# Counting the four narrowest tiles of a threshold search on GpSimd, and splitting the other ten anew

## The chip, the cores and the metric

The kernel runs on one core of a Trainium2 chip. The metric is the device time of one execution in microseconds: the median of three runs is 4006.64 us (4005.96 to 4007.17).

## The reference, cut to what matters

One inference step of a decoder layer. Part of it is a sparse attention: for every one of the prompt's 2048 queries a score is computed for each earlier key, and only the 256 keys with the highest scores are attended.

```python
score = jnp.einsum('bth,bths->bts', wi, jax.nn.relu(dots)).astype(jnp.float32)
causal = jnp.arange(L)[None, :] <= q_pos[:, None]
score = jnp.where(causal[None], score, -jnp.inf)
vals, sel = lax.top_k(score, topk)          # topk = 256
valid = vals > -jnp.inf
```

A second group of queries (8 sequences of 8 queries, the samples) attends 256 of 8192 cached positions; its keys and values are gathered from a paged cache. The layer also has a gated linear recurrence, projections and an MLP, which this change leaves alone.

## The kernel before

**How the search works.** The prompt's queries lie in 16 tiles of 128, one query per partition. The scores of tile i are a row of (i+1) x 128 columns in `score` (float32, in SBUF). The first two tiles need no selection. For the other 14 (widths 384 to 2048) the kernel looks, for each query, for the largest float whose bits, set one by one from the top, still leave at least 256 scores at or above it. That takes 32 rounds (`ROUNDS`). In each round every tile is compared with its candidate and the hits are counted; then the bit is kept or dropped, and the next candidate is formed.

Two engines count. VectorE does it in one `tensor_scalar` (`is_ge`, with the sum as `accum_out`, L2865). ACT does it in one `activation` with `Sign` and the sum (L2788). `split_search` divides the tiles by a cost table: VectorE has the widths 2048, 1792, 1536, 1280, 896, 640, 512 (8704 columns), ACT 1920, 1408, 1024, 384, 1664, 1152, 768 (8320 columns). The tiles lie in two halves, `GROUPS`. When a half is counted, VectorE's `update(r, g)` waits for both engines' counts, keeps or drops the bit (L2848, L2849), writes the candidates of the next round (L2851) and raises `cand_rdy[g]`. So one half is counted while the other is updated.

**What it is interleaved with.** The 32 rounds run inside `attend_sample_and_search_prompt`, which attends the samples. It goes over four pairs of sequences in five phases. Each phase has 16 steps (`NCK`). In a step TensorE turns key rows (L2681), multiplies queries by them (L2689), adds a mask (L2696), turns the probabilities of the pair before (L2718) and multiplies them by the values (L2732). Phase 0 has no probabilities yet and phase 4 has no keys any more. ACT copies every turned block out of PSUM (L2802) and takes the exponentials (L2809); VectorE moves the logits out with their maximum (L2907).

Each engine has its own program in order. The search is a generator in each of them. The list `STEPS` (10.0 for the start, then 5.4, 6.6 and 4.9 per step) says how much of the 32 rounds stands in each step: `step_of(position)` gives the step of a position counted in rounds, and `search_until(step)` issues all counts that are due up to that step. Counted so, phase 0 holds 5.62 rounds, phases 1 to 3 hold 6.87 each, and phase 4 holds 5.10.

**GpSimd's queue.** GpSimd has only the gathers of key and value rows (L2646), 64 in all, into four key buffers and four value buffers. A key gather waits until TensorE has turned the rows that lay in its buffer (`t_done`), and a value gather until TensorE has multiplied by its own (`t_used`, which `logits` and `times_v` raise, and `times_new` doesn't).

The stage behind, `mark_prompt_and_recur_sample`, uses the same split of tiles. There VectorE first counts ACT's tiles again, against the next float above (L1757), before ACT marks the chosen keys.

## Time and profile before

| | |
|---|---|
| median of three runs | 4006.64 us |
| the profiled execution | 4005.41 us |
| its span | 4003.6 us |
| TensorE, VectorE, ACT, GpSimd busy | 3559.9, 2780.9, 2215.1, 1054.2 us |
| stage of the search, first to last count | 1349 to 1818 us |
| L2865, VectorE's counts, over the span | 328.5 us |
| L2788, ACT's counts, over the span | 286.4 us |

The span is the time from the first to the last instruction of the profiled execution; the execution itself took 1.8 us more. Busy times of different engines overlap. A line such as L2865 is a line of the kernel before. A releaser ("<-ACT turned L2802") is what ended an engine's idle time. GpSimd is called POOL in the rows, and VectorE DVE.

### The profile page before, as it was taken

How to read it: one execution, taken by the hardware profiler on the slowest of the kernel's cores; microseconds unless marked ns; L12 is line 12 of the kernel's file. 1: busy time of each engine (PE TensorE's matmuls, PEld its weight loads, DVE VectorE, ACT ScalarE, POOL GpSimd, SP SyncE). 2: the span in 40 equal slices, each digit the busy share in tenths (PEclk: the TensorE clock that was granted, in tenths of full speed). 3: DMA queues.
4: the chain of work that ended last, by engine and by line, in shares of the span. 5: the costliest groups of instructions: out<-in, count | busy, mean ns of one | idle time of the engine just before them, and what ended most of it. 6: DMA issues, size and time to landing. Idle time of an engine off the chain costs nothing. (4 is left out here: it accounts for less than half of the span.)

```text
span 4003.6 us, 53467 instructions
## 1 busy us (share of the span) xinstructions
PE 3559.9 (89%) x18410; PEld 2847.4 (71%) x18411; DVE 2780.9 (69%) x4729; ACT 2215.1 (55%) x3701; POOL 1054.2 (26%) x1140
## 2 busy tenths in 40 slices
PE   8999999879777489874699999979999998999998
PEld 7778787778555245453588887868888887888886
DVE  6675756878888789798678885665565554555565
ACT  4343424766678599897577774345455443433232
POOL 0000001755210011110256730216555551000011
PEclk9999999999878699995799999989999999999999
DMA  6555454555100244423456633576677666554464
GB/s 169 180 149 163 144 162 128 156 152 145 44 22 16 93 153 164 159 97 117 126 196 226 233 133 130 201 238 198 200 229 225 187 192 189 184 179 152 137 218 137
DMA packets 394575, 633.11 MB, mean 158 GB/s; under 512 B 98073, under 2 KB 220793, under 8 KB 386009
## 3 DMA queue, kind: packets, MB, share of 16 engines
q1 hardware_dynamic: 314712, 314.14, 26.3%
q0 software_dynamic: 79200, 315.79, 23.7%
q8 instruction: 138, 2.26, 0.2%
q14 instruction: 109, 0.89, 0.1%
q10 hardware_dynamic: 416, 0.02, 0.0%
HBM read 448.87 MB, written 180.96 MB: 157 GB/s over the span
## 5 line engine op out<-in xcount | busy, mean ns | idle before, releaser
L3890 PE MATMUL up_acc<-x_parts_first,w_up_parts 128*128 128x512 f32 x1536 | 358.7, 393 | 15.1 <-DVE w_up_parts L3638 15.1
L775 PE MATMUL accumulated<-hT,w_in_parts 128*128 128x512 f32 x1536 | 360.4, 394 | 3.2 <-DVE w_in_parts L509 3.2
L3890 PEld LDWEIGHTS up_acc<-x_parts_first,w_up_parts 128*128 128x128 f32 x1536 | 291.4, 190 | 77.0 <-DVE w_up_parts L3638 16.0
L775 PEld LDWEIGHTS accumulated<-hT,w_in_parts 128*128 128x128 f32 x1536 | 289.9, 190 | 66.2 <-DVE w_in_parts L509 4.9
L2865 DVE TENSOR_SCALAR_CACHE_REDUCE junk_dve<-score,candidate 128x2048 bf16<-128x2048 f32 (+6 forms) x224 | 328.5, 1505 | 8.8 <-DVE candidate L2851 8.3
L3983 PE MATMUL down_acc<-w_down_parts_even,hidden_parts 128*128 128x512 f32 x1344 | 316.6, 393 | 13.2 <-DVE hidden_parts L3674 10.8
L3983 PE MATMUL down_acc<-w_down_parts_odd,hidden_parts 128*128 128x512 f32 x1344 | 312.7, 390 | 0.0
L3983 PEld LDWEIGHTS down_acc<-w_down_parts_even,hidden_parts 128*128 128x128 f32 x1344 | 254.6, 190 | 67.8 <-issue 14.8
L2788 ACT ACTIVATE junk_act<-score,candidate 128x1920 bf16<-128x1920 f32 (+6 forms) x224 | 286.4, 1294 | 21.2 <-DVEq L2852 17.4
L3436 ACT ACTIVATE hidden_parts<-hidden_raw 128x1024 fp32r<-128x1024 f32 x112 | 118.6, 1059 | 311.7 <-PE down_acc L3983 289.5
L3983 PEld LDWEIGHTS down_acc<-w_down_parts_odd,hidden_parts 128*128 128x128 f32 x1344 | 251.9, 188 | 53.1 <-issue 1.0
L357 ACT ACTIVATE w_in_parts<-w_in_raw 128x1024 fp32r<-128x1024 f32 (+1 forms) x112 | 113.6, 1014 | 290.7 <-PE accumulated L771 120.9
L509 DVE TENSOR_TENSOR w_in_parts<-w_in_raw,w_in_parts 128x1024 fp32r<-128x1024 f32 (+1 forms) x112 | 130.8, 1169 | 198.1 <-ACT w_in_parts L357 197.1
L3638 DVE TENSOR_TENSOR w_up_parts<-up_raw,w_up_parts 128x512 fp32r<-128x512 f32 x224 | 176.0, 786 | 113.8 <-ACT w_up_parts L3414 112.3
L771 PE MATMUL accumulated<-w_in_parts,hT 128*128 128x512 f32 (+1 forms) x1152 | 239.4, 366 | 1.7 <-DVE hT L530 1.7
L2173 DVE TENSOR_TENSOR probs_T<-p_T,probs_T 128x512 fp32r<-128x512 f32 x272 | 183.9, 688 | 72.6 <-ACT probs_T L2097 71.3
L771 PEld LDWEIGHTS accumulated<-w_in_parts,hT 128*128 128x128 f32 x1152 | 200.2, 188 | 32.2 <-issue 3.2
L3674 DVE TENSOR_TENSOR hidden_parts<-hidden_raw,hidden_parts 128x1024 fp32r<-128x1024 f32 x112 | 138.1, 1233 | 112.3 <-ACT hidden_parts L3436 112.0
L2097 ACT ACTIVATE probs_T<-p_T 128x512 fp32r<-128x512 f32 x272 | 157.0, 594 | 94.0 <-PE p_T L2033 93.0
L1449 PE MATMUL dots<-ki_high,qi_parts 128*128 128x512 f32 (+3 forms) x304 | 146.5, 483 | 70.0 <-ACT relu L1471 68.2
L3333 POOL DMA_DIRECT2D hidden_raw<-scratch_hs x112 | 59.8, 534 | 538.1 <-DVE hidden_parts L3674 538.1
L1518 DVE SCALAR_TENSOR_TENSOR score<-relu,wi,score 128x1024 f32<-128x1024 f32 (+7 forms) x154 | 180.5, 1172 | 24.7 <-ACT relu L1471 7.6
(556 smaller groups left out, 8655.7 us busy)
## 6 DMA issues: line engine op xcount, KB each, us to landing
hidden_raw<-scratch_hs POOLq DMA_DIRECT2D x112, 512.0 KB, 4.5
w_in_raw<-in_w_in SPq DMA_DIRECT2D x80, 512.0 KB, 4.1
up_raw<-scratch_ws SPq DMA_DIRECT2D x128, 256.0 KB, 3.0
scratch_hs<-hidden_even POOLq DMA_DIRECT2D x112, 256.0 KB, 4.9
scratch_hs<-hidden_odd POOLq DMA_DIRECT2D x112, 256.0 KB, 4.8
up_raw<-in_w_up SPq DMA_DIRECT2D x96, 256.0 KB, 5.7
weight_sums<-in_w_down POOLq DMA_DIRECT2D x16, 1024.0 KB, 5.3
scratch_wt<-weight_sums POOLq DMA_DIRECT2D x16, 1024.0 KB, 5.8
```

The costliest lines, as they stand in the source:

```text
L771: mm = pe.matmul(z, h[:, a, k, n * P:(n + 1) * P], w2[:, g % 2, b, k2 * w:(k2 + 1) * w], start=(first and j == 0), stop=(last and j == 2))
L775: mm = pe.matmul(z, w2[:, g % 2, b, k2 * ST + n * P:k2 * ST + (n + 1) * P], h[:, a, k, :], start=(first and j == 0), stop=(last and j == 2))
L1449: pe.matmul(dots[:, u % DB, c:c + w], qs[:, b, h, :], kh[:, k], start=True, stop=False)
L1518: dve.scalar_tensor_tensor(s, r, wi[:, i, h:h + 1], s, ALU.mult, ALU.add).then_inc(acc_done, 1)
L2097: act.activation(ET[:, s % 3, 0, :], pT[:, turn_at[s] % 3, :], ACT.Copy).then_inc(th_rdy, 1)
L2173: dve.tensor_tensor(ET[:, s % 3, 1, :], pT[:, turn_at[s] % 3, :], ET[:, s % 3, 0, :].bitcast(F32), ALU.subtract).then_inc(tl_rdy, 1)
L2788: act.activation(ja[:, n % 2, 0:WIDTH[i]], score[:, SOFF[i]:SOFF[i + 1]], ACT.Sign, bias=cf[:, c:c + 1], accum_out=cnt[:, c:c + 1]).then_i ...
L2865: dve.tensor_scalar(jd[:, n % 2, 0:WIDTH[i]], score[:, SOFF[i]:SOFF[i + 1]], cf[:, c:c + 1], None, ALU.is_ge, ALU.add, accum_out=cnt[:, c: ...
L3638: dve.tensor_tensor(out, raw[:, g % RAW, :], high.bitcast(F32), ALU.subtract).then_inc(lo_rdy, 1)
L3674: dve.tensor_tensor(ap[:, s % A_PARTS, 1, :], araw[:, s % A_RAW, :], ap[:, s % A_PARTS, 0, :].bitcast(F32), ALU.subtract).then_inc(a_lo, 1)
L3890: mm = pe.matmul(up_bank(n), wp[:, n % SLOTS, b, q * P:(q + 1) * P], X(i)[:, a, q, :], start=(q == 0 and (a, b) == (0, 0)), stop=(q == QUA ...
L3983: mm = pe.matmul(down_bank(s), ap[:, s % A_PARTS, a, j * P:(j + 1) * P], B(ph)[:, j, b, :], start=(j == 0 and (a, b) == (0, 0)), stop=(j = ...
```

## The change

The four narrowest tiles (768, 384, 640 and 512 columns, in this order) go to GpSimd. [...] It writes the comparison's zeros and ones as bf16 (`reaches_pool`), adds the right half of the row to the left half, halves what is left again, and writes the last sum, 64 to 96 columns wide, to `counts_pool`. VectorE's `update` reduces these to a count with a new `tensor_reduce`, in both halves. The other ten tiles are split by a new cost rule: ACT gets 2048, 1792, 1920 and 1664 (7424 columns), VectorE 1536, 1408, 1280, 1152, 1024 and 896 (7296 columns). In GpSimd's program the counts that are due up to a step stand ahead of the key gather that waits for that step.

```diff
+POOL_TILES = 4
 def split_search():
-    cost, mine = {"dve": 4400.0, "act": 5500.0}, {"dve": [], "act": []}
-    for i in sorted(SEARCHED, key=lambda i: -WIDTH[i]):
-        t = {"dve": 1.12 * WIDTH[i] + 110, "act": 0.97 * WIDTH[i] + 190}
-        who = min(t, key=lambda e: cost[e] + t[e])
-        cost[who] += t[who]
-        mine[who].append(i)
-    return mine["dve"], mine["act"][0::2] + mine["act"][1::2]
+    narrow = sorted(SEARCHED, key=lambda i: WIDTH[i])[:POOL_TILES]
+    pool = narrow[-1:] + narrow[:1] + narrow[1:-1][::-1]
+    wide = sorted((i for i in SEARCHED if i not in pool), key=lambda i: -WIDTH[i])
+
+    def share(n):
+        return max(3850 + sum(0.833 * WIDTH[i] + 308 for i in wide[:n]),
+                   2800 + sum(1.042 * WIDTH[i] + 209 for i in wide[n:]))
+
+    n = min(range(2, len(wide) - 1), key=share)
+    return wide[n:], wide[:n][0::2] + wide[:n][1::2], pool
...
+        ADDED = (slice(0, half_pt), slice(NSRCH - half_pt, NSRCH))
+        ENDS = {i: WIDTH[i] >> (3 if WIDTH[i] >= 512 else 2) for i in PT}
+        reaches = sb("reaches_pool", [P, max(WIDTH[i] for i in PT)], BF16)
+        part = sb("counts_pool", [P, len(PT), max(ENDS.values())], BF16)
...
+                link_p = Chain(pool, chain_p)
+
+                def counts():
+                    link_p(pool.memset(part[:, :, :], 0.0))
+                    for r in range(ROUNDS):
+                        for m, i in enumerate(PT):
+                            yield step_of(r + m / len(PT))
+                            c, w = col[i], WIDTH[i]
+                            if m % half_pt == 0:
+                                pool.wait_ge(cand_rdy[m // half_pt], r + 1)
+                            pool.wait_ge(p_cnt, len(PT) * r + m)
+                            link_p(pool.tensor_scalar(reaches[:, 0:w], score[:, SOFF[i]:SOFF[i + 1]], cf[:, c:c + 1], None, ALU.is_ge))
+                            while w > 2 * ENDS[i]:
+                                w //= 2
+                                link_p(pool.tensor_tensor(reaches[:, 0:w], reaches[:, 0:w], reaches[:, w:2 * w], ALU.add))
+                            w //= 2
+                            pool.tensor_tensor(part[:, m, 0:w], reaches[:, 0:w], reaches[:, w:2 * w], ALU.add).then_inc(p_cnt, 1)
...
                 for n in range(4 * NS + 2 * LASTP):
+                    if n >= KB:
+                        pair, c, s = place(n - KB)
+                        search_until(NCK * pair + 4 * c + 3)
                     if n < 4 * NS:
                         if n >= KB:
-                            pair, c, s = place(n - KB)
                             pool.wait_ge(t_done, ev_k(pair, 4 * c + 3, s) + 1)
...
+                search_until(len(STEPS) - 1)
...
                     dve.wait_ge(a_cnt, na * r + (n1, na)[g])
+                    dve.wait_ge(p_cnt, len(PT) * r + half_pt * (g + 1))
+                    link_c(dve.tensor_reduce(cnt[:, ADDED[g]], part[:, half_pt * g:half_pt * (g + 1), :], AX.X, ALU.add))
```

`Chain` raises a semaphore with each instruction and waits for it, so each of GpSimd's instructions waits for the one before. In the rows below, GpSimd's lines are L2646 for a gather before, and after the change L2657 for a gather, L2670 for the compare, L2673 for a halving and L2675 for the last addition of a tile.

GpSimd at the end of the stage, before: the last gathers follow each other with nothing between them.

```order
L2646 DMA k_rows<-in_cache_k,gather_kv 128x2048
L2646 DMA v_rowsS<-in_cache_v,gather_kv 128x2048
L2646 DMA k_rows<-in_cache_k,gather_kv 128x2048
L2646 DMA v_rowsS<-in_cache_v,gather_kv 128x2048
```

And after the change, the last two gathers (of value rows) with the end of the counts in front of them and the beginning of those behind them.

```order
L2673 TENSOR_TENSOR reaches_pool<-reaches_pool 128x192
L2675 TENSOR_TENSOR counts_pool<-reaches_pool 128x96
L2670 TENSOR_SCALAR reaches_pool<-score,candidate 128x384
L2673 TENSOR_TENSOR reaches_pool<-reaches_pool 128x192
L2675 TENSOR_TENSOR counts_pool<-reaches_pool 128x96
L2657 DMA v_rowsS<-in_cache_v,gather_kv 128x2048 x2
L2670 TENSOR_SCALAR reaches_pool<-score,candidate 128x640
L2673 TENSOR_TENSOR reaches_pool<-reaches_pool 128x320
L2673 TENSOR_TENSOR reaches_pool<-reaches_pool 128x160
L2675 TENSOR_TENSOR counts_pool<-reaches_pool 128x80
L2670 TENSOR_SCALAR reaches_pool<-score,candidate 128x512
```

The gathers now stand between counts. Of the last three pairs of value gathers, the first has 5 tiles' counts behind it up to the second, the second 5 up to the third, and the third 10 up to the end: 20 tiles, which are 5 rounds. A pair of key and value gathers in the phases before has 6 or 7 tiles' counts up to the next group of four gathers.

VectorE over one round in phase 0, before, between two of the maxima of L2907.

```order
L2907 TENSOR_SCALAR logitsS,z_max<-zL 128x512
L2865 TENSOR_SCALAR junk_dve,count<-score,candidate 128x1280
L2848 TENSOR_TENSOR kept<-count,least_count 128x7
L2849 COPY_PREDICATED F<-kept,candidate 128x7
L2851 TENSOR_TENSOR candidate<-F,bits_p 128x7
L2865 TENSOR_SCALAR junk_dve,count<-score,candidate 128x896
L2907 TENSOR_SCALAR logitsS,z_max<-zL 128x512
```

And the same place after the change, where L2948 is the maximum, L2906 a count and L2881 the new reduction.

```order
L2948 TENSOR_SCALAR logitsS,z_max<-zL 128x512
L2881 TENSOR_REDUCE count<-counts_pool 128x2
L2889 TENSOR_TENSOR kept<-count,least_count 128x6
L2890 COPY_PREDICATED F<-kept,candidate 128x6
L2892 TENSOR_TENSOR candidate<-F,bits_p 128x6
L2906 TENSOR_SCALAR junk_dve,count<-score,candidate 128x1152
L2906 TENSOR_SCALAR junk_dve,count<-score,candidate 128x1024
L2948 TENSOR_SCALAR logitsS,z_max<-zL 128x512
```

The update begins with the reduction of GpSimd's partial sums, so VectorE's queue now also waits for GpSimd there; the maxima stand behind it.

## Rows read from the trace of the kernel before

**Rows 1.** The page's chain that ended last, by line.

```profile
PE down_acc L3983 15%; PE up_acc L3890 14%; PE out_acc L3956 4%; PE sample_acc L3915 1%; PE mix_turned L3859 0%; PE sample_acc L3931 0%; PE sample_turned L3931 0%; DVE x_parts_first L3638 0%; PE rows_turned L3868 0%; DMA down_raw<-scratch_wt 0%; DMA hidden_raw<-scratch_hs 0%; DVE x_parts_last L3638 0%; DMA up_raw<-scratch_ws 0%; PE sample_turned L3902 0%; DMA scratch_xc<-normed_T 0%
```

**Rows 2.** Busy time by stretch: the five phases (start:end, length, engines).

```profile
1363.00:1443.60 80.60, 62.89 (x225) 24.61 (x225) 68.81 (x144) 62.01 (x103) 11.24 (x12) 0.85 0.43 156
1443.60:1541.90 98.30, 88.90 (x546) 51.10 (x546) 88.18 (x178) 93.14 (x153) 14.72 (x16) 0.97 0.41 150
1541.90:1642.50 100.60, 90.71 (x563) 52.44 (x560) 89.27 (x183) 92.88 (x153) 12.44 (x14) 0.97 0.44 165
1642.50:1754.30 111.80, 92.55 (x547) 51.83 (x545) 88.77 (x180) 93.42 (x151) 12.18 (x13) 0.94 0.34 123
1754.30:1818.70 64.40, 44.57 (x329) 35.95 (x329) 60.21 (x118) 61.23 (x98) 5.62 (x6) 0.84 0.27 99
```

**Rows 3.** Timeline of TensorE, value products of two successive steps (start, us).

```profile
1522.76 1.58 PE L2732 MATMUL zO<-v_rowsS,turned 128*64 128x128 f32 x16
...
1528.21 1.58 PE L2732 MATMUL zO<-v_rowsS,turned 128*64 128x128 f32 x16
```

**Rows 4.** Timeline of TensorE at a phase's end (in brackets: idle before).

```profile
1541.63 0.43 PE L2745 MATMUL zO<-v_new,turned 8*64 8x128 f32 x4 [3.15 <-ACT turned L2802]
```

**Rows 5.** Waits in the stage: us in total, times, longest.

```profile
PE zL L2689 <- ACT turned L2802: 36.8, 28, 4.0
```

**Rows 6.** Groups by form in the stage, counts (busy us, mean ns).

```profile
L2865 DVE TENSOR_SCALAR_CACHE_REDUCE junk_dve<-score,candidate 128x2048 bf16<-128x2048 f32 x32 | 74.9, 2342 | 0.3 <-DVE candidate L2856 0.3
...
L2865 DVE TENSOR_SCALAR_CACHE_REDUCE junk_dve<-score,candidate 128x512 bf16<-128x512 f32 x32 | 23.7, 742 | 0.0
...
L2788 ACT ACTIVATE junk_act<-score,candidate 128x1920 bf16<-128x1920 f32 x32 | 60.9, 1905 | 18.2 <-DVEq L2852 14.5 <-DVEq L2858 3.7
...
L2788 ACT ACTIVATE junk_act<-score,candidate 128x384 bf16<-128x384 f32 x32 | 20.0, 626 | 0.0
```

**Rows 7.** The same view, VectorE's reduction of 128 elements.

```profile
L2925 DVE TENSOR_REDUCE z_max<-logitsS 128x1 f32<-128x128 f32 x4 | 1.1, 286 | 0.1
```

**Rows 8.** Timeline of VectorE: first instruction of an update, and the count behind it.

```profile
1523.79 0.17 DVE L2848 TENSOR_TENSOR kept<-count,least_count 128x7 int32<-128x7 f32 x1
...
1524.53 1.15 DVE L2865 TENSOR_SCALAR_CACHE_REDUCE junk_dve<-score,candidate 128x896 bf16<-128x896 f32 x1 [0.17 <-DVE candidate L2851]
```

**Rows 9.** GpSimd's instructions elsewhere (min/median/max ns; memsets: busy us, ns).

```profile
L1424 POOL CAST qi_parts<-qi_rows x12: 1040/1142/1728, 1024.5 to 1247.1; 128x1024 fp32r<-128x1024 f32 x12
...
L1948 POOL TENSOR_TENSOR weight_sums<-weight_sums x16: 1272/1282/1294, 1979.2 to 2168.7; 128x512 f32<-128x512 f32 x16
...
L1426 POOL TENSOR_TENSOR qi_parts<-qi_rows,qi_parts x12: 2363/2572/3096, 1025.7 to 1248.6; 64x1024 fp32r<-64x1024 f32 x12
...
L989 POOL TENSOR_TENSOR less_ref<-r_b,b_less_log_k x96: 620/836/1280, 684.5 to 862.9; 128x256 f32<-128x256 f32 x96
...
L1620 POOL MEMSET minus_twos<- 128x2048 bf16 x1 | 1.8, 1795 | 0.0
...
L994 POOL MEMSET qi_blocks<- 128x1024 f32 x1 | 0.9, 945 | 0.0
...
L995 POOL MEMSET ki_new<- 128x64 f32 x1 | 0.1, 145 | 0.0
```

**Rows 10.** Timeline of GpSimd: two additions of which the second waits for the first.

```profile
1981.72 1.28 POOL L1961 TENSOR_TENSOR weight_sums<-weight_sums 128x512 f32<-128x512 f32 x1
1983.08 1.29 POOL L1963 TENSOR_TENSOR weight_sums<-weight_sums 128x512 f32<-128x512 f32 x1
```

**Rows 11.** Timeline of GpSimd: gathers of value rows in the last phase.

```profile
1764.40 0.94 POOL L2646 DMA_INDIRECT v_rowsS<-in_cache_v,gather_kv  x1 [27.86 <-PE zO L2732]
1765.64 0.94 POOL L2646 DMA_INDIRECT v_rowsS<-in_cache_v,gather_kv  x1 [0.30 <-issue]
...
1799.33 0.94 POOL L2646 DMA_INDIRECT v_rowsS<-in_cache_v,gather_kv  x1 [13.74 <-PE zO L2732]
```

**Rows 12.** Timeline of ACT in the stage behind: its first mark.

```profile
1841.01 0.72 ACT L1673 ACTIVATE sides<-score,minus_last 128x512 bf16<-128x512 f32 x1
```

More of the change, by code:

```diff
@@ L1267, with search_columns @@
 SOFF = [o - OFF[FIRST] for o in OFF]
+POOL_TILES = 4
 def split_search():
-    cost, mine = {"dve": 4400.0, "act": 5500.0}, {"dve": [], "act": []}
-    for i in sorted(SEARCHED, key=lambda i: -WIDTH[i]):
-        t = {"dve": 1.12 * WIDTH[i] + 110, "act": 0.97 * WIDTH[i] + 190}
-        who = min(t, key=lambda e: cost[e] + t[e])
-        cost[who] += t[who]
-        mine[who].append(i)
-    return mine["dve"], mine["act"][0::2] + mine["act"][1::2]
-def search_columns(dt, at):
-    nd0 = (len(dt) - 1) // 2
-    return nd0, dt[:nd0] + at + dt[nd0:]
+    narrow = sorted(SEARCHED, key=lambda i: WIDTH[i])[:POOL_TILES]
[6 more added lines that the diff above has]
+    return wide[n:], wide[:n][0::2] + wide[:n][1::2], pool
+def search_columns(dt, at, pool):
+    nd0, half = (len(dt) - 1) // 2, len(pool) // 2
+    return nd0, half + nd0, pool[:half] + dt[:nd0] + at + dt[nd0:] + pool[half:]
 PROBS_SKIP = 136000
@@ L1537, in mark_prompt_and_recur_sample @@
     LV = 3
-    DT, AT_ = split_search()
-    nd, columns = search_columns(DT, AT_)
+    DT, AT_, PT = split_search()
+    _, nd, columns = search_columns(DT, AT_, PT)
     ACTS = slice(nd, nd + len(AT_))
@@ L2564, in attend_sample_and_search_prompt @@
         o_done, o_rdy, out, chain = sem("z_o"), sem("z_or"), sem("z_out"), sem("z_chain")
-        DT, AT_ = split_search()
-        nd, na = len(DT), len(AT_)
+        DT, AT_, PT = split_search()
+        nd, na, half_pt = len(DT), len(AT_), len(PT) // 2
         n1 = -(-na // 2)
-        nd0, columns = search_columns(DT, AT_)
+        nd0, a0, columns = search_columns(DT, AT_, PT)
         col = {i: n for n, i in enumerate(columns)}
-        GROUPS = (slice(0, nd0 + n1), slice(nd0 + n1, NSRCH))
-        SIGNED = (slice(nd0, nd0 + n1), slice(nd0 + n1, nd0 + na))
+        GROUPS = (slice(0, a0 + n1), slice(a0 + n1, NSRCH))
+        SIGNED = (slice(a0, a0 + n1), slice(a0 + n1, a0 + na))
+        ADDED = (slice(0, half_pt), slice(NSRCH - half_pt, NSRCH))
+        ENDS = {i: WIDTH[i] >> (3 if WIDTH[i] >= 512 else 2) for i in PT}
+        reaches = sb("reaches_pool", [P, max(WIDTH[i] for i in PT)], BF16)
+        part = sb("counts_pool", [P, len(PT), max(ENDS.values())], BF16)
+        p_cnt, chain_p = sem("z_p_cnt"), sem("z_chain_p")
         F, flip = keep["F"], keep["flip"]
@@ L2647, in gather, with search_until @@
                                             bass.IndirectOffsetOnAxis(ap=gkv[:, 2 * pair + s, c:c + 1], axis=0)).then_inc(done[g % nb], 16)
+                link_p = Chain(pool, chain_p)
[14 more added lines that the diff above has]
+                            pool.tensor_tensor(part[:, m, 0:w], reaches[:, 0:w], reaches[:, w:2 * w], ALU.add).then_inc(p_cnt, 1)
+                search = counts()
+                due = [next(search)]
+                def search_until(step):
+                    while due[0] <= step:
+                        due[0] = next(search, len(STEPS))
                 for n in range(4 * NS + 2 * LASTP):
+                    if n >= KB:
+                        pair, c, s = place(n - KB)
+                        search_until(NCK * pair + 4 * c + 3)
                     if n < 4 * NS:
                         if n >= KB:
-                            pair, c, s = place(n - KB)
                             pool.wait_ge(t_done, ev_k(pair, 4 * c + 3, s) + 1)
@@ L2872, in rounds @@
                     update(ROUNDS - 1, 1)
-                    link_c(dve.tensor_tensor(F[:, nd0:nd0 + na], F[:, nd0:nd0 + na], bitn[:, 31:32].to_broadcast([P, na]), ALU.bitwise_xor))
+                    link_c(dve.tensor_tensor(F[:, a0:a0 + na], F[:, a0:a0 + na], bitn[:, 31:32].to_broadcast([P, na]), ALU.bitwise_xor))
                 search = rounds()
@@ L4021, in constants @@
     second = np.stack([np.tile(a, (1, RH)) for a in halves], 1).astype(np.int32)
-    dt_, at_ = split_search()
-    least = [2 * TOPK - 1 - WIDTH[i] if i in at_ else TOPK for i in search_columns(dt_, at_)[1]]
+    dt_, at_, pt_ = split_search()
+    least = [2 * TOPK - 1 - WIDTH[i] if i in at_ else TOPK for i in search_columns(dt_, at_, pt_)[2]]
     bits = np.array([1 << b for b in range(30, -1, -1)] + [0], np.uint32)
```

## The prediction

> **What bounds the kernel now.** I read the chain of waits first: its two longest items are lines of the MLP at the kernel's end, far from this change [rows 1]. Nothing there alters, so the change is worth what the stage that holds the search, `attend_sample_and_search_prompt`, becomes shorter or longer, and everything behind it shifts. Then I cut that stage into five stretches at the ends of its pair phases [rows 2]. By the table STEPS they hold 5.62, 6.87, 6.87, 6.87 and 5.10 search rounds (0.65 lies before, hidden by the loads of the queries). The reader is to see that no engine has room: in the three middle stretches VectorE is busy for 88 to 89 us, ACT for 93 and TensorE for 89 to 93, of 98.3, 100.6 and 111.8.
>
> The timeline of TensorE gives its floor: one middle step, from one block of 16 value products to the next, takes 5.45 us with no gap [rows 3]. Sixteen steps are 87.2 us; the idle gaps at a phase's end (3.15 us before its last product [rows 4], about as long again for the first exponential) lift that to about 94.5. So TensorE alone forbids a middle stretch under 94.5, and the most the change could save there is 4 + 6 + 17 = 27 us. The last two stretches are long because TensorE waits for ACT's copies: 36.8 us in the stage before L2689 alone [rows 5].
>
> The table by form gives the counts [rows 6]. VectorE: 2342 ns at 2048 columns and 742 at 512, so 1.042 ns a column and 209 ns; the next starts 0.075 us early, at the accumulator read. ACT: 1905 at 1920 and 626 at 384, so 0.833 ns a column and 306 ns.
>
> **The change part by part.** VectorE counts 7296 columns in 6 instructions instead of 8704 in 7: 10.5 - 0.5 = 10.0 us a round become 8.86 - 0.45 = 8.4. Each of the two updates a round gains one reduction of 2 x 96 elements. One over 128 elements took 286 ns [rows 7]; at 1.04 ns an element this is 0.36 us, 0.40 with the gap, 0.8 a round. The update itself takes 0.74 us, from 1523.79 to 1524.53 [rows 8], as before. VectorE's round goes from 11.5 to 10.7. ACT counts 7424 columns in 4 instructions instead of 8320 in 7: 9.0 us become 7.4.
>
> In the second stretch VectorE's busy 88.2 us lose 6.87 x 0.8 = 5.5 and become 83, and ACT's 93.1 lose 6.87 x 1.65 = 11 and become 82 [rows 2]. Both fall well under TensorE's 94.5.
>
> GpSimd gets 15 instructions a round, none of a kind seen in this trace. Compares: 4 over 2304 columns with one input. The nearest rows are the cast, 1040 ns at least over 1024, and the memsets, 145 ns over 64 and 945 over 1024 [rows 9]: 0.833 ns a column and 0.19 us each, 2.7 us. Adds: 11 over 1968 columns with two inputs. A row of 512 columns takes 1282 ns; at 2.50 ns a column and nothing fixed they are 4.9 us. Through it and 2363 ns (1024 columns of half the partitions) the line is 2.11 a column and 0.2 us, 6.35 in all. I take 5.8, since something fixed is in every row. Each instruction waits for the one before; such a pair stood 0.08 us apart, from 1983.00 to 1983.08 [rows 10]: 1.2 us. A round is 9.7 us. From both sides: adds at the one-input rate give 3.7 and a round of 7.6; compares at the two-input rate give 5.7 and a round of 13.2. I take 9.7 because the cast is the nearest row to a compare.
>
> The Trainium skill (GPSIMD Engine Reference, Performance pitfalls for Q7 kernels) says that a body that produces a truth value costs 2.03 cycles an element if it isn't unrolled and 1.03 if it is. The trace has only the cast's rate. At its 1.2 GHz that would be, as an estimate, 1.7 ns a column, and a round of 11.7 us.
>
> GpSimd also issues the gathers, 1.24 us each from start to start [rows 11]. Four middle steps hold 1.72 rounds and 4 gathers: 1.72 x 9.7 + 5.0 = 21.7 us against 24 of a quarter stretch. It fits, with 2 us to spare. But the queue is in order, and that is the new wait. Before a key gather stand all counts up to that step; behind it a value gather waits until TensorE has used its buffer, and behind that wait stand the counts of the next four steps. VectorE's update waits for them, and behind it in its queue stand the maxima that TensorE's logits need, and the candidates that ACT waits for. In the second stretch the value gather is free about 2 us after VectorE enters the last step that GpSimd has counted for, so nothing is lost. `times_new` doesn't raise `t_used`, so each later phase's gathers are released one event later: in the third and fourth stretches by logits of the following step. There GpSimd starts its counts about 3 us late; its quarter stays at 24 to 25 us.
>
> Sum by stretch. First: VectorE's 5.62 rounds lose 0.8 each, and GpSimd's 5.62 x 9.7 + 12 x 1.24 = 69.4 us fit into 76; 80.6 becomes 76, -4.5. Second: TensorE's floor and 1.5 us, -2.3. Third: 97.5, -3. Fourth: ACT's share of a step falls by 0.43 x 1.65 = 0.7 us, 16 of them 11 us, of which the late counts take 1: -10.
>
> Last stretch: here the queue costs. By the rows the gathers left at 10.1 us into it (1764.40) and at 45.0 us (1799.33), in step with TensorE [rows 11], and VectorE searched on meanwhile. Now the first of them has exactly 5 rounds of counts behind it (order shown with the change: 5 tiles, 5 tiles, 10 tiles). From 10.1 us on GpSimd needs 5 x 9.7 = 48.5 us, 6 gathers of 1.24, 7.4 us, and sits out two waits in which ACT alone goes on for up to 0.64 rounds. In the first ACT has two tiles to count once the second half's candidates are there, then a copy and the product: 3.4 us after GpSimd is done. In the second ACT needs one tile more, 5.0 us. With the final update 0.8: 75.2 us against 64.4, +10.8.
>
> Total: -4.5 - 2.3 - 3 - 10 + 10.8 = -9. The stage behind counts ACT's tiles again, 4 instead of 7; ACT started its marks there at 1841.01 with no idle time before it [rows 12], behind its own activations and not behind these counts, so I take 0. `memset` of the partial sums ahead of the first gather, some 0.4 us by the memsets' line, hides behind the load of the queries. The profiled execution took 4005.4 us (span 4003.6); the median is 4006.6, 1.2 above. So 3996.4 + 1.2: 3997 us.
>
> **Rivals.** (a) GpSimd is cheap, 8 us a round, since bf16 adds may be nearer to the one-input rate. The stretches save 5, 3.3, 5 and 13 us and the last loses only 10.8 - 5.3 x 1.7 = 1.8: 3982. For it: the output and inputs of the adds are half as wide as in any row. Against: the bf16 memset ran at the f32 memset's rate.
> (b) Slower: GpSimd becomes the bound. The place is its quarter of a middle stretch; it decides from (24 - 5) / 1.72 = 11 us a round. At 12 us a quarter is 25.6 and a middle stretch 102.4 + 3 for the phase's end: +7, +5 and -6; the first +3, the last 10.8 + 5.3 x 2.3 = +23. Total +32: 4039. For it: compares have no row, and all 15 instructions wait on each other. Against: it needs compares at nearly twice the cast's rate.
> (c) GpSimd and VectorE hold each other up. L989 took 620 ns at least, 836 as median and up to 1280 [rows 9], so other work can stretch it by a third. All of GpSimd's work a third longer is 8.5 x 1.35 + 1.2 = 12.7 us a round, +50: 4057. Against: VectorE's counts read one tensor at one column per 1.04 ns, and L1948 stayed at 1272 to 1294 ns for all 16. The Trainium skill (GPSIMD Engine Reference, Key points) puts contention on VectorE instructions in a two-port mode or with two SBUF inputs; by that rule only the small ones of the updates would meet it.
> (d) Gains and the loss at the end cancel within the measurement: 4006.
>
> **How the numbers follow.** What a measurement tells from no change is 0.2%, 8 us. The forecast, 0.45, has 3984 to 4012 as its own range, since the four savings rest on waits that could each be off by 2 to 3 us: 0.28 of it faster, 0.12 same, 0.05 slower. (a) 0.17, faster. (b) 0.26, slower. (c) 0.07, slower. (d) 0.05, same. Together faster 0.45, same 0.17, slower 0.38. The range goes from 3972, a little under (a), to 4045, a little over (b); the bound of 13.2 us a round, some +65 us, stays outside with most of (c).
>
> **What would show it.** GpSimd's instructions from one 768-column compare to the next, without gathers: 9.7 us, compares 0.83 and adds about 2.3 ns a column. VectorE 8.4 and ACT 7.4 us of counts a round. Three middle stretches of 96 to 102 us with TensorE's gaps before L2689 in the stage under 25 us. A last stretch of about 75 us, ended by GpSimd's counts, with VectorE idle before the new reductions. If that stretch is no longer than 65 us, the step on the queue is wrong; if a round of GpSimd is over 11 us, the price is.

## The result and the profile after

The changed kernel took 4086.58 us (median of 4 runs, 4083.68 to 4096.2) against 4006.89 of the kernel before on the same chip (4005.96 to 4007.17): 1.0202 times as long (95% interval 1.0189 to 1.0216). Forecast were 3997 us in a range of 3972 to 4045. The change makes the kernel slower by 80 us, more than the 50 of the dearest rival, and the time lies outside the range. A GpSimd round over 11 us was named as the sign that the price is wrong; it is 14.05 us, as shown below. The profiled execution took 4083.68 us, 78.3 more than the one before, with a span of 4081.9 and a mean granted clock of 0.93 (0.937 before).

The five stretches of the stage in the changed kernel, cut as in [rows 2] (start:end, length, then busy us of PE, PEld, DVE, ACT and POOL, the granted clock, DMA share and GB/s):

```profile
1363.00:1447.30 84.30, 60.68 (x225) 23.68 (x223) 67.20 (x144) 55.11 (x73) 72.45 (x87) 0.86 0.28 105
1447.30:1563.10 115.80, 95.45 (x554) 53.66 (x554) 86.40 (x179) 82.65 (x111) 102.39 (x119) 0.88 0.38 146
1563.10:1679.70 116.60, 94.36 (x554) 52.49 (x554) 86.88 (x182) 83.43 (x112) 102.86 (x121) 0.91 0.38 145
1679.70:1794.10 114.40, 90.59 (x549) 51.09 (x547) 87.98 (x183) 83.16 (x111) 101.11 (x120) 0.97 0.34 130
1794.10:1893.60 99.50, 48.07 (x325) 39.14 (x325) 59.99 (x116) 53.97 (x65) 71.97 (x85) 0.71 0.18 64
```

The stage starts at the same 1363.00, and its five stretches are 3.7, 17.5, 16.0, 2.6 and 35.1 us longer: 74.9 of the 78.3. ACT lost the 10 us a stretch that it was meant to lose (93.1 to 82.7 in the second), and is no bound. The engine that has filled up is GpSimd: 102 busy us of 116, where it had 12 to 15; most of the rest are the gaps of about 0.09 us between instructions that wait for each other. The granted clock of the second stretch fell from 0.97 to 0.88 and that of the last from 0.84 to 0.71, while TensorE waited more; the second stretch holds nearly the same matmuls (554 and 546 records), and their busy time rose from 88.90 to 95.45 us. The fourth stretch is nearly as long (114.4 us) with the clock at 0.97 and 90.59 busy us, so the clock isn't what makes these stretches long.

One round of GpSimd without a gather, from one compare of 768 columns to the next (start, us):

```profile
1350.22 2.21 POOL L2670 TENSOR_SCALAR reaches_pool<-score,candidate 128x768 bf16<-128x768 f32 x1 [0.16 <-issue]
1352.52 1.53 POOL L2673 TENSOR_TENSOR reaches_pool<-reaches_pool 128x384 bf16<-128x384 bf16 x2
...
1364.27 2.20 POOL L2670 TENSOR_SCALAR reaches_pool<-score,candidate 128x768 bf16<-128x768 f32 x1 [0.17 <-POOL counts_pool L2675]
```

It takes 14.05 us, not 9.7. The groups by form say which part of it is dearer (busy us, mean ns | idle before):

```profile
L2670 POOL TENSOR_SCALAR reaches_pool<-score,candidate 128x768 bf16<-128x768 f32 x32 | 70.5, 2203 | 4.9 <-POOL counts_pool L2675 4.6 <-issue 0.2
...
L2670 POOL TENSOR_SCALAR reaches_pool<-score,candidate 128x384 bf16<-128x384 f32 x32 | 39.8, 1244 | 2.8
...
L2673 POOL TENSOR_TENSOR reaches_pool<-reaches_pool 128x384 bf16<-128x384 bf16 x32 | 29.2, 912 | 2.7
```

The additions are as forecast: 5.7 us a round, where I took 5.8. Through the two compares the line is (2203 - 1244) / 384 = 2.50 ns a column and 0.28 us fixed; all of them are 220.6 us x128, so 6.9 us a round. Forecast were 2.7, from a line through the cast's 1040 ns with the memsets' slope of 0.833 ns a column [rows 9]. That alone is 4.2 of the 4.35 us that a round is longer.

The waits of the stage (us in total, times, longest) name what follows from it:

```profile
ACT junk_act L2827 <- DVEq L2893: 117.3, 48, 9.5
...
DVE count L2881 <- POOL counts_pool L2675: 114.9, 39, 9.9
...
PE zL L2728 <- ACT turned L2841: 68.0, 31, 7.4
```

VectorE waits 115 us for the partial sums, ACT 117 for the new candidates that VectorE gives out only then, and TensorE's wait for ACT's copies went from 36.8 [rows 5] to 68.0. The last shows under ACT's name. But in ACT's program the copies stand behind its counts, and the counts waited for candidates: whoever reads only the last releaser would blame the engine that was relieved.

### The profile page after: what moved, and what is told of

The parts are those of the page before. It is cut to its first block and busy times, and to the rows that moved or that the text cites. A ratio compares the mean times of both kernels' runs of the same rounds, so it can differ in the third digit from the quotient of the medians.

```text
span 4081.9 us, 53818 instructions
## 1 busy us (share of the span) xinstructions
PE 3565.5 (87%) x18411; PEld 2846.9 (70%) x18411; DVE 2772.5 (68%) x4723; ACT 2168.7 (53%) x3509; POOL 1462.6 (36%) x1621
## 3 DMA queue, kind: packets, MB, share of 16 engines
q0 software_dynamic: 79200, 315.79, 23.1%
## 5 line engine op out<-in xcount | busy, mean ns | idle before, releaser
L2827 ACT ACTIVATE junk_act<-score,candidate 128x2048 bf16<-128x2048 f32 (+3 forms) x128 | 235.1, 1838 | 121.1 <-DVEq L2893 117.3
L2906 DVE TENSOR_SCALAR_CACHE_REDUCE junk_dve<-score,candidate 128x1536 bf16<-128x1536 f32 (+2 forms) x192 | 276.9, 1476 | 7.0 <-DVE candidate L2892 6.5
L2670 POOL TENSOR_SCALAR reaches_pool<-score,candidate 128x768 bf16<-128x768 f32 (+3 forms) x128 | 220.6, 1723 | 18.2 <-POOL counts_pool L2675 8.9
L2728 PE MATMUL zL<-turned,q_blocks 128*64 128x512 f32 x256 | 151.3, 692 | 73.5 <-ACT turned L2841 68.0
```

Of the source, the lines that this page charges most:

```text
L2670: link_p(pool.tensor_scalar(reaches[:, 0:w], score[:, SOFF[i]:SOFF[i + 1]], cf[:, c:c + 1], None, ALU.is_ge))
L2728: pe.matmul(lp[half(s), n % 2, :], qb[:, 2 * pair + s, :], turned[:, e % TB, :], start=True, stop=False, skip_group_check=True).then_inc(t ...
L2827: act.activation(ja[:, n % 2, 0:WIDTH[i]], score[:, SOFF[i]:SOFF[i + 1]], ACT.Sign, bias=cf[:, c:c + 1], accum_out=cnt[:, c:c + 1]).then_i ...
L2906: dve.tensor_scalar(jd[:, n % 2, 0:WIDTH[i]], score[:, SOFF[i]:SOFF[i + 1]], cf[:, c:c + 1], None, ALU.is_ge, ALU.add, accum_out=cnt[:, c: ...
```

## The experiments

Two theories stood at first. **A**: a compare is slow by itself on GpSimd. **B** (rival): it is slow because VectorE reads the same scores beside it, as in rival (c). And a second question: would the forecast hold if the compare had the price that I gave it?

**e1_alone: the forms of instruction with VectorE standing still.** Ahead of the counts GpSimd runs nine forms at 768 and at 384 columns, and VectorE starts its search only behind them. Added; nothing is left out, and the total says nothing:

```
+ for w in (768, 384):
+     row = score[:, 0:w]
+     link_p(pool.tensor_scalar(reaches[:, 0:w], row, thr[:, 0:1], None, ALU.is_ge))
+     ... # against a constant, subtract, f32 output, bf16 input, add and multiply,
+     ... # a copy, bf16 addition, f32 addition
+ pool.sem_inc(alone, 1)
  ...
+ dve.wait_ge(alone, 1)
```

> The changed kernel with 18 extra GpSimd instructions ahead of the first gather, while VectorE, ACT and TensorE wait: nine forms at 768 and at 384 columns, each behind the one before. Theory: GpSimd's compare costs 2.5 ns a column by itself, 2.20 us at 768 and 1.24 us at 384 as in the changed kernel, and a plain copy about 0.83 to 1.0 ns a column; then the price that failed is the comparison's (or that of any one-input arithmetic: subtract at 2.5 as well would say that). Rival, contention with VectorE: alone the compare takes 1.5 us or less at 768. The total time of this run says nothing but for its extra 15 to 30 us.

Timeline of GpSimd: compare, subtract, add and multiply by constants, copy; then the compare of 384:

```profile
1353.05 2.21 POOL L2668 TENSOR_SCALAR reaches_pool<-score,least_count 128x768 bf16<-128x768 f32 x1
...
1357.58 2.21 POOL L2670 TENSOR_SCALAR reaches_pool<-score,least_count 128x768 bf16<-128x768 f32 x1
...
1364.47 0.83 POOL L2673 TENSOR_SCALAR reaches_pool<-score 128x768 bf16<-128x768 f32 x1
1365.37 0.82 POOL L2674 CAST reaches_pool<-score 128x768 bf16<-128x768 f32 x1
...
1369.89 1.25 POOL L2668 TENSOR_SCALAR reaches_pool<-score,least_count 128x384 bf16<-128x384 f32 x1
```

2.21 us alone (VectorE is idle from 1348.88 to 1379.85 us) against 2.203 in the kernel, 1.25 against 1.244: the price is the instruction's own, and contention on GpSimd's side is out. Theory A held. It isn't a matter of types either (bf16 input 2.20, f32 output 2.21), nor of the truth value, since a subtraction costs the same; against a constant it is 2.13.

**e7_forms: is it the column of scalars, or the number of operations?** e1 left open why one form of the same instruction ran at 0.83. The same place, with nine other forms:

```
+ tensor_scalar(..., row, thr[:, 0:1], 1.0, ALU.is_ge, ALU.mult)
+ tensor_scalar(..., row, thr[:, 0:1], 2.0, ALU.subtract, ALU.mult)
+ tensor_scalar(..., row, 2.0, thr[:, 0:1], ALU.mult, ALU.add)
+ tensor_scalar(..., row, 0.5, thr[:, 0:1], ALU.add, ALU.mult)
+ tensor_scalar(..., row, 2.0, None, ALU.mult)
+ ... # four more
```

> As e1_alone, with other forms of GpSimd's tensor_scalar at 768 and 384 columns: two operations in one instruction (compare and multiply, subtract and multiply, multiply and add, subtract and compare) and one multiplication. In e1_alone one operation cost 2.5 ns a column whatever it was, but add and multiply with two constants 0.85. Theory A: it is the number of operations, and compare with a multiplication by 1 is fast too, about 0.83 us at 768. Theory B: only multiply with add has a fast path, and every form with a compare stays at 2.2 us at 768.

Timeline of GpSimd, the five forms above in their order:

```profile
1350.56 2.86 POOL L2668 TENSOR_SCALAR reaches_pool<-score,least_count 128x768 bf16<-128x768 f32 x1
...
1356.39 2.86 POOL L2670 TENSOR_SCALAR reaches_pool<-score,least_count 128x768 bf16<-128x768 f32 x1
1359.35 0.91 POOL L2671 TENSOR_SCALAR reaches_pool<-score,least_count 128x768 bf16<-128x768 f32 x1
...
1363.31 0.90 POOL L2673 TENSOR_SCALAR reaches_pool<-score,least_count 128x768 bf16<-128x768 f32 x1
...
1367.25 2.15 POOL L2675 TENSOR_SCALAR reaches_pool<-score 128x768 bf16<-128x768 f32 x1
```

Neither. A multiplication and an addition together, in either order, run at the cast's rate, even with a column of scalars. Every other form that was tried is slow, a single multiplication too (2.15), and a compare or a subtraction with a second operation takes 2.86. A single addition was not tried. A compare has no form among those tried that runs at the rate I assumed.

**e2_short_compare: the round at the price that I had forecast.** Each compare reads only `ENDS` of its tile's columns (64 to 96, the width at which the additions end), so that the round is near 9.7 us with every instruction, wait and addition in place. Left out: the rest of the four narrowest tiles' columns; their thresholds come from an eighth to a quarter of them, and the number of hits asked for is scaled to that. The last addition of a tile takes the short compare's output as one input. The core of the edit:

```
- link_p(pool.tensor_scalar(reaches[:, 0:w], score[:, SOFF[i]:SOFF[i + 1]], ..., ALU.is_ge))
+ e = ENDS[i]
+ link_p(pool.tensor_scalar(some[:, 0:e], score[:, SOFF[i]:SOFF[i] + e], ..., ALU.is_ge))
```

> The changed kernel with GpSimd's compares cut to the last sum's width (64 to 96 columns instead of 384 to 768), all additions left in and the least counts scaled to it; so the four narrowest tiles get thresholds from a part of their columns. GpSimd's round falls from 14.0 to about 9.1 us, near the 9.7 of the prediction. Theory (only the price of the compare was wrong): the stretches come out as the prediction's sum, the middle ones 96 to 102 us, the last about 73, and the total 3990 to 4003. Rival (the queue with the gathers, or the new wait of the update, costs by itself): middle stretches stay over 104 us, and the total over 4012.

Busy time by stretch, second to last:

```profile
1440.70:1536.80 96.10, 89.85 (x554) 51.82 (x554) 82.74 (x178) 82.47 (x111) 67.72 (x118) 0.96 0.46 173
1536.80:1632.60 95.80, 89.85 (x552) 51.78 (x553) 84.32 (x183) 83.35 (x111) 68.83 (x121) 0.96 0.47 176
1632.60:1738.80 106.20, 91.43 (x550) 51.35 (x548) 85.95 (x183) 82.89 (x111) 64.94 (x115) 0.95 0.38 140
1738.80:1821.90 83.10, 44.44 (x325) 36.15 (x325) 59.28 (x116) 53.90 (x65) 44.69 (x81) 0.79 0.21 77
```

Its round is 9.1 us, 0.6 under the 9.7 of the forecast. 4010.30 us, ratio 1.0011 (1.0001 to 1.0020). So the price of the compare is worth about 76 us of the 80 lost. But the kernel doesn't get to 3997 either, nor into the 3990 to 4003 expected of this run: neither theory came out whole. The second and third stretches are as forecast (96.1 and 95.8 for 96 and 97.5) with TensorE's clock back at 0.96; the fourth is 4 us over (106.2 for 102), and the last, forecast at 75.2 with a longer round, is 83.1.

**e3_two_tiles: half of it moved.** `POOL_TILES = 4` becomes 2: GpSimd counts only the tiles of 512 and 384 columns, ACT five and VectorE seven. Nothing is left out.

> The changed kernel with two tiles (512 and 384 columns) on GpSimd instead of four; ACT then has five tiles with 8960 columns, VectorE seven with 7168. GpSimd's round is about 5.9 us by the measured instructions (3.3 + 2.5), a quarter of a middle stretch 15 us of 24, so it is no bound. Theory: VectorE's round is 8.4 + 1.5 + 0.6 = 10.5 us instead of 11.5, ACT's stays at 8.9; the time comes back to 3990 to 4012, with a last stretch lengthened by the gathers' waits by some 3 us. Rival (any count behind the gathers costs): over 4020.

The last two stretches:

```profile
1633.20:1745.40 112.20, 94.84 (x554) 53.53 (x554) 81.79 (x193) 92.16 (x124) 46.48 (x59) 0.92 0.36 132
1745.40:1818.60 73.20, 44.90 (x329) 36.03 (x329) 56.39 (x131) 62.53 (x78) 31.61 (x41) 0.86 0.24 87
```

4003.61 us, ratio 0.9994 (0.9982 to 1.0005): the loss is gone, a gain isn't there. That is inside the expected 3990 to 4012. The last stretch is 8.8 us longer than before, where 3 were expected. The fourth still is 112 us, as in the kernel before.

**e4_count_new_rows: the release that comes late.** The prediction said that `times_new` does not raise `t_used`, so that the gathers of the third to fifth stretches leave one to three events late. Something that it didn't name waits on the same count: ACT's copies of turned blocks, which go into four slots of `turned` (`act.wait_ge(t_used, e - TB + 1)`, just above L2802). They too are released late. This puts the missing count behind `times_new(phase - 1)` in the kernel *before*, with nothing else changed:

```
+ pe.wait_ge(o_done, phase)
+ pe.sem_inc(t_used, 1)
```

> The kernel before, in which TensorE also raises t_used once its products with the new rows are done (a wait for o_done and a raise, behind times_new). Theory (from the prediction: the third to fifth stretches are lengthened because every later phase's copies and gathers are released one event late): the fourth stretch falls from 111.8 to about 100 us, the last from 64.4 to about 61, the total to 3988 to 3996. Rival (ACT's own work sets those stretches and the late releases are harmless): within 3 us of the kernel before.

```profile
1641.50:1740.00 98.50, 89.63 (x554) 51.55 (x553) 88.26 (x180) 92.16 (x153) 11.45 (x13) 0.97 0.38 140
1740.00:1802.80 62.80, 43.25 (x325) 35.06 (x325) 60.04 (x119) 60.38 (x95) 3.75 (x4) 0.84 0.26 94
```

The fourth stretch falls from 111.8 to 98.5 with ACT as busy as ever. TensorE's wait for ACT's copies in the stage falls with it:

```profile
PE zL L2689 <- ACT turned L2804: 23.1, 20, 4.0
```

36.8 became 23.1 us. Which of the two releases it was, the waits in the fourth stretch alone say. In the kernel before, ACT's copies stood still there, with turned blocks ready for them, until TensorE had used a slot:

```profile
ACT turned L2802 <- PE zL L2689: 16.7, 16, 3.7
```

In e4 that row is gone from the stretch, and in neither kernel does TensorE show a wait for gathered rows there. So in this stretch the copies' release cost the time, and not the gathers'. No run raises the count for one of the two alone. 3989.80 us, ratio 0.9954 (0.9940 to 0.9967): the kernel before was itself losing about 17 us to this count (16.4 by the medians, 18 by the ratio).

**e5, e6, e8: the same two lines on e2, on e3 and on the changed kernel.** They ask whether the rest of the last stretch is the queue order together with the late release. What was expected of e5, e6 and e8, in this order:

> The short compares of e2_short_compare together with e4_count_new_rows. Theory: with cheap compares what was lost in the last stretch (83 us measured in e2_short_compare against 64 before) is GpSimd waiting for value gathers that are released one to three events late, with the counts queued behind them. Then the last stretch falls to 60 to 66 us, the fourth to 96 to 100, the total to 3978 to 3988, under both parts alone. Rival: the last stretch is long because the counts by themselves don't fit, whatever the gathers do: it stays over 74 us, and the total over 3992.

> Two tiles on GpSimd (e3_two_tiles) together with e4_count_new_rows; nothing is left out, so this is a candidate for a version that beats both kernels. Theory: e3_two_tiles had GpSimd idle most of the time, its last stretch was 73 us for the same late gathers; now 61 to 64, the fourth 97 to 100, total 3978 to 3988. Rival: two tiles bring nothing of their own: total within 3 us of e4_count_new_rows, 3987 to 3993.

> The changed kernel, complete, with e4_count_new_rows. GpSimd's round stays at 14.0 us, its quarter of a middle stretch at 5.0 + 1.72 x 14.0 = 29.1 us. Theory: the three middle stretches stay at 114 to 117 us, since GpSimd is their bound and never waits there; the last one loses the 18.5 us that GpSimd sat waiting for value gathers and goes from 99.5 to 80 to 84; total 4066 to 4072. Rival (the late releases, not the round, made the middle stretches long): they fall under 108 us and the total under 4050.

Last two stretches of e5, the last of e8, the last three of e6:

```profile
1629.30:1726.00 96.70, 89.50 (x554) 51.56 (x552) 84.16 (x183) 82.14 (x111) 66.72 (x117) 0.96 0.41 155
1726.00:1787.20 61.20, 42.80 (x325) 34.64 (x325) 58.18 (x117) 52.75 (x65) 42.67 (x80) 0.82 0.28 102
```

```profile
1797.90:1879.50 81.60, 48.69 (x325) 40.19 (x325) 60.08 (x117) 53.30 (x65) 72.06 (x85) 0.71 0.22 78
```

```profile
1529.80:1626.20 96.40, 89.05 (x549) 51.17 (x549) 82.24 (x197) 93.10 (x127) 50.69 (x66) 0.96 0.47 176
1626.20:1720.90 94.70, 89.05 (x554) 51.35 (x553) 80.75 (x192) 91.61 (x125) 47.43 (x61) 0.96 0.42 156
1720.90:1783.50 62.60, 43.20 (x325) 35.50 (x325) 56.25 (x131) 60.26 (x75) 30.49 (x40) 0.81 0.28 102
```

e5 took 3973.76 us, 0.9918 (0.9905 to 0.9932), 4 us under the expected 3978; its last stretch is 61.2 for e2's 83.1, inside the expected 60 to 66. Value gathers of that stretch in e2, then in e5 (in brackets the wait):

```profile
1750.26 1.03 POOL L2658 DMA_INDIRECT v_rowsS<-in_cache_v,gather_kv  x1 [13.70 <-PE zO L2774]
...
1771.80 1.03 POOL L2658 DMA_INDIRECT v_rowsS<-in_cache_v,gather_kv  x1 [7.44 <-PE zO L2774]
...
1792.64 1.03 POOL L2658 DMA_INDIRECT v_rowsS<-in_cache_v,gather_kv  x1 [7.74 <-PE zO L2774]
```

```profile
1743.85 1.03 POOL L2658 DMA_INDIRECT v_rowsS<-in_cache_v,gather_kv  x1 [2.81 <-PE zO L2774]
...
1757.08 1.03 POOL L2658 DMA_INDIRECT v_rowsS<-in_cache_v,gather_kv  x1 [0.15 <-POOL counts_pool L2678]
```

With the counts queued behind them, waits of 13.7 and 7.4 us are 2.8 and 0.15 once the release comes in time. e8, with compares at their true price, gains 17.9 us in the last stretch and nothing in the three before (115.8, 116.7, 114.3): there GpSimd is the bound, and no release helps it. It took 4063.62 us, 1.0143 (1.0126 to 1.0160), 2 us under the expected 4066.

**e6 is complete and beats both kernels**: 3969.73 us, ratio to the kernel before 0.9910 (0.9895 to 0.9925). Its three middle stretches, 94.7 to 96.4 us, stand at TensorE's floor of about 94.5. Against e4, which has the two lines alone, it is 18 us faster by the ratios and 20 by the medians (the two ran on different chips), and 8 us under the expected 3978. So the version with two tiles on GpSimd is worth having, and the one with four, which is e8, is not. How much of the 18 to 20 us is the columns that GpSimd took over, and how much the other split between VectorE and ACT that came with it, no run separates.

**e9_fast_form_added: the round set to the rival's point.** Two theories were left for the 20 us by which e2 and the changed kernel differ in a middle stretch: the length of GpSimd's round, or something peculiar to the slow compare. To e2 one fast multiply-and-add over each tile's whole width is added, so that the round is near 12 us without slow compares of whole tiles. Left out is what e2 leaves out; besides, the last addition of a tile adds the short compare's output to itself, and the hits asked for are doubled for that. The core of the edit:

```
+ link_p(pool.tensor_scalar(reaches[:, 0:w], reaches[:, 0:w], 0.0, thr[:, c:c + 1], ALU.mult, ALU.add))
```

> The short compares of e2_short_compare with one multiply-and-add instruction of the tile's whole width added in front of each (0.9 us at 768 columns in e7_forms); as there, the four narrowest tiles get thresholds from a part of their columns. GpSimd's round becomes 9.1 + 3.0 = about 12.2 us, a quarter 5.0 + 1.72 x 12.2 = 26 us against TensorE's 24. Theory (the quarter is the bound beyond 11 us a round): middle stretches of 103 to 106 us and a total of 4035 to 4050. Rival (GpSimd's work disturbs VectorE and so costs even below its bound, or the gathers' order does): the middle stretches are over 109 us. It also tells which instruction of GpSimd stretches the first of VectorE's update: 0.40 us as in the changed kernel if any long one does, about 0.21 as in e2_short_compare if only the compare does.

Its second and last stretch:

```profile
1444.90:1549.40 104.50, 93.17 (x554) 52.94 (x554) 86.89 (x179) 82.61 (x111) 87.91 (x148) 0.93 0.43 161
...
1762.30:1852.30 90.00, 45.81 (x325) 37.43 (x325) 58.82 (x117) 54.03 (x65) 61.37 (x106) 0.75 0.20 71
```

The round is 12.45 us, the middle stretches 104.5, 105.2 and 107.7, the total 4038.70 us (ratio 1.0090, 1.0073 to 1.0107). The total and two of the three stretches are where the theory put them; the third is 1.7 over its 106 and still under the rival's 109. So the length of the round, and not the slow compare as such, sets the middle stretches.

## Why the prediction was wrong

**The step that failed is the price of GpSimd's compares**: "0.833 ns a column and 0.19 us each, 2.7 us", taken "because the cast is the nearest row to a compare". They cost 2.50 ns a column and 0.28 us, 6.9 us a round (compares alone, e1: the same). The row was nearest only in having one input and one output; the trace held no row that priced the operation. The bound from the other side, compares at the rate of the two-input additions, gave 5.7, and with the dearer additions the round of 13.2; even that was under the measured 14.05, and I left it out of the range. The Trainium skill (GPSIMD Engine Reference, Performance pitfalls for Q7 kernels) puts a body that makes a truth value at 2.03 cycles an element if it isn't unrolled, against 1.03; my estimate from it was a round of 11.7 us. It pointed the right way, in part by luck: the measured price is above it, and a plain subtraction, which makes no truth value, cost the same 2.21 us at 768 columns (e1).

**The mechanism of rival (b) is what happened**, at 14.05 us a round instead of 12. Its formula, a quarter of a middle stretch is 5.0 + 1.72 x round, gives 29.2 us and four of them 116.7; measured were 115.8, 116.6 and 114.4. At e9's 12.45 it gives 4 x 26.4 = 105.6; measured 104.5, 105.2, 107.7. The 3 us that (b) added for the phase's end are not in these stretches. At e2's 9.1 it is under TensorE's 24 and the stretch is TensorE's 96. So the point from which it decides, 11 us, is bracketed by e2 and e9. The chance that I gave it was 0.26. Rival (b)'s whole total, 4039 at 12 us, was met by e9 with 4038.7, but partly by luck: e9's round is 0.45 us longer, which makes up for the 3 us.

**The last stretch.** The formula 10.1 + 5 rounds + 7.4 + 3.4 + 5.0 + 0.8 gives 97 at 14.05 us; measured 99.5. The changed kernel's gathers there, and its end on VectorE:

```profile
1805.76 1.03 POOL L2657 DMA_INDIRECT v_rowsS<-in_cache_v,gather_kv  x1 [8.54 <-PE zO L2771]
...
1829.81 1.03 POOL L2657 DMA_INDIRECT v_rowsS<-in_cache_v,gather_kv  x1 [3.41 <-PE zO L2771]
...
1855.04 1.03 POOL L2657 DMA_INDIRECT v_rowsS<-in_cache_v,gather_kv  x1 [6.53 <-PE zO L2771]
```

```profile
1892.60 0.35 DVE L2881 TENSOR_REDUCE count<-counts_pool 128x2 f32<-128x192 bf16 x1 [2.42 <-POOL counts_pool L2675]
```

The first gather leaves 11.7 us into the stretch, where 10.1 was taken from [rows 11], the two later ones are waited for as described (3.41 and 6.53 us; 3.4 and 5.0 were allowed), and the last update waits for GpSimd. At short rounds the formula is too low, though: at 9.1 us it gives 72.2, and e2 took 83.1. The gathers' waits are the reason: in e2 the first leaves after 11.5 us, and the two later ones wait 7.44 and 7.74, together 15.2 where I allowed 8.4. With these the formula gives 80.4. So even if compares cost what I gave them, the time would not have been 3997 but about 4010 (e2): by the formula at e2's round the last stretch was undersized by 11 us, and the fourth by 4. The sum itself comes to 3997.6, which was written as 3997.

**The late release** was seen and named for the gathers only, and priced as 1 us of ACT's gain; that ACT's copies wait on the same count was overlooked. By e4 it cost the kernel before 13 us in the fourth stretch, where it held the copies, and by e2 and e5 it was 9.5 us in the fourth and 22 in the last, where the gathers' waits above held the counts behind them. The forecast saving of 10 us in the fourth stretch was put down to ACT's shorter counts, and [rows 5] was read as ACT having too much to do; e4 shows that the same stretch was long for another reason, with ACT's work untouched. ACT's shorter counts brought 5.6 us there (106.2 in e2) and, with the release in time, 1.8 (96.7 in e5 for 98.5 in e4).

**Right as forecast:** TensorE's floor of 94.5 (94.0 to 96.7 in the middle stretches of e5 and e6); additions 5.7 for 5.8; the new reduction 351 ns for 0.36 us; ACT's 10.5 us less in the second stretch for 11. The first stretch took 84.3 us: GpSimd's 87 instructions in it are 12 gathers and 75 counts, so 5 rounds, and 5 x 14.05 + 12 x 1.24 = 85.1, where 5.62 rounds had been put there. The stage behind was put at 0: ACT's first mark there comes 23.7 us after the stage's end (1917.30) against 22.3 before, so 1.4. The other 2 us outside the five stretches were not traced.

**Missed, and small: VectorE's update was stretched.** "As before" was wrong. Its first instruction took 163 ns in the kernel before (62 times) and in the changed one

```profile
L2889 DVE TENSOR_TENSOR kept<-count,least_count 128x6 int32<-128x6 f32 x31 | 12.8, 412 | 1.1
```

and 385 ns for the other half: 14.6 us more over the stage. That is most of why VectorE's busy time in the second stretch is 86.4 us and not the forecast 83. So rival (c) was half right: nobody slows GpSimd's compares, but GpSimd slows VectorE, mostly in this one tiny instruction with two inputs. The four additions of 128x128, two inputs as well, went from 296 to 493 ns, the instructions behind the first in an update by up to 31 ns; the counts stayed as they were. The Trainium skill (GPSIMD Engine Reference, Key points) puts the contention just there, and the traces agree. The same instruction took 207 ns in e2, with short compares, and in e9, with the fast form over whole tiles,

```profile
L2894 DVE TENSOR_TENSOR kept<-count,least_count 128x6 int32<-128x6 f32 x31 | 11.5, 372 | 1.1
```

It isn't the slow compare that does it, since e9 has none over a whole tile. Nor does VectorE sit out the whole of GpSimd's instruction, as one might think. Two updates of the changed kernel, one soon after a compare has begun and one later in it, and one of e9:

```profile
1465.65 2.20 POOL L2670 TENSOR_SCALAR reaches_pool<-score,candidate 128x768 bf16<-128x768 f32 x1 [0.17 <-POOL counts_pool L2675]
1466.00 0.57 DVE L2889 TENSOR_TENSOR kept<-count,least_count 128x8 int32<-128x8 f32 x1
...
1498.54 2.20 POOL L2670 TENSOR_SCALAR reaches_pool<-score,candidate 128x768 bf16<-128x768 f32 x1 [0.17 <-POOL counts_pool L2675]
1499.68 0.17 DVE L2889 TENSOR_TENSOR kept<-count,least_count 128x8 int32<-128x8 f32 x1
```

```profile
1507.19 0.91 POOL L2674 TENSOR_SCALAR reaches_pool<-reaches_pool,least_count 128x768 bf16<-128x768 bf16 x1 [0.18 <-POOL counts_pool L2680]
1507.53 0.58 DVE L2894 TENSOR_TENSOR kept<-count,least_count 128x8 int32<-128x8 f32 x1
```

In both kernels the held instruction ends 0.92 us after the one of GpSimd began. In e9 that is GpSimd's end; the compare goes on for 1.3 us more. Beside compares of 640 columns it ends after 0.81 us (their length is 1.88, the fast form's 0.80), and an update that begins 1.1 us or more into a compare of 768 columns takes its 0.17 us. So a compare holds VectorE for no longer than the fast form of the same width, whatever its own length. That it reads its input in this time and then only computes would fit, but was not tried. In the changed kernel these 14.6 us cost little: GpSimd, the bound, waited only 2.9 us in the whole stage for new candidates.

What stays open: why a single multiplication costs 2.15 us on GpSimd and a multiplication with an addition 0.91 at the same size; the runs show that it is so and not why. Nor was the split with three tiles on GpSimd tried, which lies between e6 and e8.

## What to carry to other kernels

Before work is moved to an engine that the trace doesn't show doing it, measure the exact form of instruction alone; the row of a neighbouring operation can be off by a factor of 2.6. Where a rival's threshold (here 11 us a round) lies inside the bounds of the unknown price (7.6 to 13.2), the range has to reach what the upper bound gives. Work appended to an in-order queue of gathers inherits every wait in that queue, so first look whether the buffers are released as early as they could be, and which engines wait on each release. A wait under an engine's name isn't yet that engine's load: look what it was itself waiting for. Here two lines that release the buffers in time were worth about 17 us alone, and turned the split with two tiles from no gain into 0.991 of the time before.

## What the runs showed of the hardware

- GpSimd, one input, 768 columns, f32 to bf16: cast 0.82 us; multiplication and addition in one instruction 0.83 (constants) to 0.91 (a column of scalars); compare, subtraction or multiplication by itself 2.13 to 2.21; a compare or a subtraction with a second operation 2.77 to 2.86 (e1, e7). Additions of two bf16 tensors 1.63, of f32 1.80.
- VectorE beside it: a count of 1536 columns took 1.81 us in both kernels; an instruction of 6 or 7 elements a partition with two inputs went from 163 to 412 ns. Held by a compare of 768 columns it ended 0.92 us after the compare's start, though the compare took 2.20.
- TensorE's granted clock (a mean of its two levels, 1.2 and 2.4 GHz, as a share of the upper) was lower in the second stretch the longer that was: 0.96 in e2's of 96.1 us, 0.93 in e9's of 104.5, 0.88 in the changed kernel's of 115.8. It isn't so everywhere: the changed kernel's fourth stretch, 114.4 us, had 0.97, and the same stretch of e8, 114.3 us, 0.91. The second stretch's matmuls took 89.85, 93.17 and 95.45 busy us for the same 554 records. These slower matmuls did not lengthen the stretch by themselves, as far as the fourth shows: e8's had 95.44 busy us and the changed kernel's 90.59, in the same 114 us.
